# The beginning of a two-layer encoder: input pieces, weight halves and the order of the first copies

## The reference

```
def even_layer(x, norm_w, w_in, ...):
    h = rmsnorm(x, norm_w)
    proj = einsum('bsd,de->bse', h, w_in)          # 1024 x 9216
    qa, ka, va, ga, qh, ffw, fbw, ih, gh = split_cols(proj, EVEN_SIZES)
    oa = differential_attention(qa, ka, va, ..., cos, sin) * silu(ga)   # q, k rotated first
    ob = hgrn2_bidirectional(qh, ffw, fbw, ih, ...) * silu(gh)
    return einsum('bse,ed->bsd', concat([oa, ob]), w_out)
```

## Time and profile before

| | us |
|---|---|
| median of three runs | 1117.99 |
| the profiled execution, its own time | 1119.73 |
| its span, from the first instruction to the last | 1118.0 |
| PE busy | 1093.4 (98%) |
| DVE busy | 967.5 (87%) |
| ACT busy | 678.7 (61%) |

### The profile page before, as it was taken

One profiled execution on the slowest core, in us unless ns is written; L12 is line 12 of the kernel. 1 busy time (PEld: TensorE's weight loads), 2 busy tenths in 40 slices (PEclk: granted clock), 3 DMA queues, 4 the chain that ended last, 5 costly groups with the idle time before them and its releaser, 6 DMA issues. The chain is left out here.

```text
span 1118.0 us, 18504 instructions
## 1 busy us (share of the span) xinstructions
PE 1093.4 (98%) x5690; PEld 913.1 (82%) x5690; DVE 967.5 (87%) x1956; ACT 678.7 (61%) x1310; POOL 0.2 (0%) x4
## 2 busy tenths in 40 slices
PE   8999999999999999999999999999999999999996
PEld 7778878888888888888888867878888888888876
DVE  6879989889889889889889888888888888988886
ACT  6475665654654654654654765367677666677764
POOL 0000000000000000000000000000000000000000
PEclk9999999999999999999999999999999999999998
DMA  7614423324224224225125120563332324323111
GB/s 231 167 41 106 140 76 93 96 75 101 87 75 114 74 75 125 62 75 140 47 75 150 44 71 22 124 160 97 98 94 56 94 63 121 100 75 94 57 39 76
DMA packets 132634, 103.67 MB, mean 93 GB/s; under 512 B 5488, under 2 KB 118512, under 8 KB 132592
## 3 DMA queue, kind: packets, MB, share of 16 engines
q1 hardware_dynamic: 131760, 102.28, 33.4%
q10 hardware_dynamic: 832, 0.85, 0.2%
HBM read 77.95 MB, written 2.10 MB: 72 GB/s over the span
## 5 line engine op out<-in xcount | busy, mean ns | idle before, releaser
L75 PE MATMUL bank_proj<-hH,w_hi 128*128 128x512 f32 x856 | 341.4, 399 | 1.1 <-DVE w_lo L1323 1.1
L77 PE MATMUL bank_proj<-hH,w_lo 128*128 128x512 f32 x856 | 334.4, 391 | 0.0
L76 PE MATMUL bank_proj<-hL,w_hi 128*128 128x512 f32 x856 | 334.3, 391 | 0.0
L77 PEld LDWEIGHTS bank_proj<-hH,w_lo 128*128 128x128 f32 x856 | 160.8, 188 | 34.9
L75 PEld LDWEIGHTS bank_proj<-hH,w_hi 128*128 128x128 f32 x856 | 161.2, 188 | 32.2 <-DVE w_lo L1323 2.0
L76 PEld LDWEIGHTS bank_proj<-hL,w_hi 128*128 128x128 f32 x856 | 161.2, 188 | 29.8 <-issue 0.2
L2087 ACT ACTIVATE probs<-probs,small 128x256 f32<-128x256 f32 (+1 forms) x128 | 70.9, 556 | 55.2 <-DVE small L2355 54.8
L1323 DVE TENSOR_TENSOR w_lo<-w_raw,w_hi 128x1024 fp32r<-128x1024 f32 x73 | 88.3, 1218 | 0.9 <-ACT w_hi L789 0.9
L2094 ACT ACTIVATE probsT<-bank_odd_turn 128x256 fp32r<-128x256 f32 (+1 forms) x128 | 49.0, 434 | 64.4 <-PE bank_odd_turn L1810 63.7
L789 ACT ACTIVATE w_hi<-w_raw 128x1024 fp32r<-128x1024 f32 x73 | 76.9, 1053 | 0.2
L918 ACT ACTIVATE scaled<-decay 128x1024 f32<-128x1024 f32 x32 | 34.0, 1062 | 61.8 <-PE bank_score L611 59.7
(11 more groups left out here) (463 smaller groups left out, 2157.8 us busy)
## 6 DMA issues: line engine op xcount, KB each, us to landing
w_raw<-in_w_in_even SPq DMA_DIRECT2D x71, 512.0 KB, 4.7
w_raw<-in_w_in_odd SPq DMA_DIRECT2D x36, 512.0 KB, 4.9
qs<-parts SPq DMA_DIRECT2D x96, 128.0 KB, 2.4
ks<-parts SPq DMA_DIRECT2D x40, 256.0 KB, 4.5
o_raw<-in_w_out_even SPq DMA_DIRECT2D x15, 512.0 KB, 6.3
o_raw<-in_w_out_odd SPq DMA_DIRECT2D x14, 512.0 KB, 6.7
mixT<-in_x SPq DMA_DIRECT2D x4, 256.0 KB, 6.0
rope<-in_rope SPq DMA_DIRECT2D x2, 512.0 KB, 7.5
```

Of the source, the lines that this page charges most:

```text
L75: pe.matmul(out, hi, moving_hi, start=start, stop=False)
L76: pe.matmul(out, hi, moving_lo, start=False, stop=False)
L77: return pe.matmul(out, lo, moving_hi, start=False, stop=stop)
```

## The change

The change has five parts.

1. `x` comes in five pieces instead of four: of one, one, two, two and two tiles (`PIECES`). The first four pieces of rows 256 to 511 are issued by ACT, where before it issued the first two of four.
2. On SP's queue the third weight block (`load(0, 0)`) and the rotary tables are issued only after all of `x` has landed; the block now stands ahead of the tables.
3. The dummy matmuls are spread: seven ahead of tile 0, six ahead of tile 1, four ahead of tile 2, none ahead of tile 3. Tiles 4 to 7 are each turned behind one step of the first projection, where before tiles 4 and 5 stood together behind the first step.
4. The second weight block is split to high and low in two halves (`high_half`, `low_half`), and the first projection step of n = -1 waits for the first half alone. The second half of the first block moves behind tiles 2 and 3 on ACT and DVE.
5. `rotate(-1, 7)` takes `low(0, 1)` between its fourth and its fifth instruction; before, `low(0, 1)` stood behind it.

```diff
-WARM = 9
+WARM = (7, 6, 4, 0)
+PIECES = ((0, 1), (1, 2), (2, 4), (4, 6), (6, 8))
@@ sync
             load_half(0, half_landed)
             load_x(0, 1)
+            load_x(0, 2)
             load_half(4, w_in_sem[0])
-            for i in (2, 3):
-                for a in range(2):
-                    load_x(a, i)
+            load_x(0, 3)
+            load_x(0, 4)
+            load_x(1, 4)
             load(0, -1)
+            sp.wait_ge(x_landed[-1].sem, x_landed[-1].at(0, 2))
+            load(0, 0)
             sp.dma_start(rope[:], rope_d).then_inc(rope_landed.sem, DMA)
-            load(0, 0)
@@ tensor
-            for c in range(WARM):
-                pe.matmul(PB[1][:, 0:P], ones, ones, start=True, stop=True)
             for k in range(4):
+                for c in range(WARM[k]):
+                    pe.matmul(PB[1][:, 0:P], ones, ones, start=True, stop=True)
                 turn_x(k)
@@
-            proj(0, -2, 0, 1)
-            turn_x(4)
-            turn_x(5)
-            proj(0, -2, 1, 2)
-            turn_x(6)
-            proj(0, -2, 2, 3)
-            turn_x(7)
-            proj(0, -2, 3, 4)
+            for k in range(4):
+                proj(0, -2, k, k + 1)
+                turn_x(k + 4)
             proj(0, -2, 4)
-            proj(0, -1, 0, 5)
+            proj(0, -1, 0, 4)
+            proj(0, -1, 4, 5)
@@ scalar
-            for i in range(2):
+            for i in range(4):
...
             high_x(0)
             act.wait_ge(half_landed.sem, half_landed.at(0, 1))
-            act.activation(w_hi[0][:, 0:4], w_raw[0][:, 0:4], ACT.Copy).then_inc(half_high.sem, 1)
-            high_x(1)
+            high_half(0, 0, half_high)
+            for k in range(1, 4):
+                high_x(k)
             act.wait_ge(w_in_sem[0].sem, w_in_sem[0].at(0, 0))
-            act.activation(w_hi[0][:, 4:KT], w_raw[0][:, 4:KT], ACT.Copy).then_inc(w_high.sem, 1)
+            high_half(0, 4, w_high)
+            high_x(4)
             keep_first_x()
-            for k in range(2, KT):
+            for k in range(5, KT):
                 high_x(k)
-            high(0, -1)
+            act.wait_ge(w_in_sem[1].sem, w_in_sem[1].at(0, 0))
+            high_half(1, 0, half_high)
+            high_half(1, 4, w_high)
@@ vector, rotate
                 dve.tensor_tensor(turned[:, 0], turned[:, 0], turned[:, 1], ALU.add).then_inc(roped.sem, 1)
+                if between is not None:
+                    low(*between)
@@ vector
-            rotate(-1, 7)
-            low(0, 1)
+            rotate(-1, 7, between=(0, 1))
             rotate(-1, 8)
```

More of the change, by code:

```diff
@@ L230, in even_layer @@
         KEPT = (1, 2, 5, 3, 4)
-        x_landed = [sem(f"x_landed{i}", unit=DMA) for i in range(4)]
+        x_landed = [sem(f"x_landed{i}", unit=DMA) for i in range(len(PIECES))]
         eye_landed = sem("eye_landed", unit=DMA)
@@ L334, in load_x @@
             def load_x(a, i):
-                part = x[2 * a * P:2 * (a + 1) * P, 2 * i * P:2 * (i + 1) * P].rearrange("(t p) d -> p t d", p=P)
-                sp.dma_start(x_tiles[a][:, :, 2 * i * P:2 * (i + 1) * P], part).then_inc(x_landed[i].sem, DMA)
+                cols = slice(PIECES[i][0] * P, PIECES[i][1] * P)
+                part = x[2 * a * P:2 * (a + 1) * P, cols].rearrange("(t p) d -> p t d", p=P)
+                sp.dma_start(x_tiles[a][:, :, cols], part).then_inc(x_landed[i].sem, DMA)
             def load_half(first, count):
@@ L455, in turn_x @@
                     pe.wait_ge(eye_landed.sem, eye_landed.at(0, 1))
-                if k % 2 == 0:
-                    pe.wait_ge(x_landed[k // 2].sem, x_landed[k // 2].at(0, 2))
+                for i, (first, _) in enumerate(PIECES):
+                    if k == first:
+                        pe.wait_ge(x_landed[i].sem, x_landed[i].at(0, 2))
                 if k == 6:
@@ L476, in proj @@
                 bank, use = bank_of(n)
-                if n == -2 and first == 0:
-                    pe.wait_ge(half_low.sem, half_low.at(0, 1))
-                elif first == 0 or n == -2 and first <= 4 < end:
+                if n in (-2, -1) and first == 0:
+                    pe.wait_ge(half_low.sem, half_low.at(0, n + 3))
+                elif first == 0 or n in (-2, -1) and first <= 4 < end:
                     pe.wait_ge(w_low.sem, w_low.at(h, n))
@@ L762, in _ @@
         def _(act):
-            for i in range(2):
-                part = x[2 * P:4 * P, 2 * i * P:2 * (i + 1) * P].rearrange("(t p) d -> p t d", p=P)
-                act.dma_start(x_tiles[1][:, :, 2 * i * P:2 * (i + 1) * P], part).then_inc(x_landed[i].sem, DMA)
+            for i in range(4):
+                cols = slice(PIECES[i][0] * P, PIECES[i][1] * P)
+                part = x[2 * P:4 * P, cols].rearrange("(t p) d -> p t d", p=P)
+                act.dma_start(x_tiles[1][:, :, cols], part).then_inc(x_landed[i].sem, DMA)
                 if i == 0:
@@ L1349, in _, with low_half @@
             low_x = lambda k: raw.split_low(dve, k, XB[k][:])
+            def low_half(s, first, count):
+                part = slice(first, first + 4)
+                dve.tensor_tensor(w_lo[s][:, part], w_raw[s][:, part], w_hi[s][:, part].bitcast(F32),
+                                  ALU.subtract).then_inc(count.sem, 1)
             low_x(0)
             dve.wait_ge(half_high.sem, half_high.at(0, 1))
-            dve.tensor_tensor(w_lo[0][:, 0:4], w_raw[0][:, 0:4], w_hi[0][:, 0:4].bitcast(F32),
-                              ALU.subtract).then_inc(half_low.sem, 1)
-            low_x(1)
+            low_half(0, 0, half_low)
+            for k in range(1, 4):
+                low_x(k)
             dve.wait_ge(w_high.sem, w_high.at(0, -2))
-            dve.tensor_tensor(w_lo[0][:, 4:KT], w_raw[0][:, 4:KT], w_hi[0][:, 4:KT].bitcast(F32),
-                              ALU.subtract).then_inc(w_low.sem, 1)
+            low_half(0, 4, w_low)
             keep_x(KEPT[0])
-            for k in range(2, KT):
+            for k in range(4, KT):
                 low_x(k)
-            low(0, -1)
+            dve.wait_ge(half_high.sem, half_high.at(0, 2))
+            low_half(1, 0, half_low)
+            dve.wait_ge(w_high.sem, w_high.at(0, -1))
+            low_half(1, 4, w_low)
             for k in KEPT[1:]:
```

9 lines of the change are left out of this document (6 added, 3 removed).

## The result

The change makes the kernel slower by a little under 0.2%.

| | median | lowest to highest |
|---|---|---|
| before | 1116.86 us | 1116.0 to 1119.32 |
| after | 1119.36 us | 1117.94 to 1121.44 |

The account below looks back on a forecast made before the run. PE, busy 98% of the span, was taken to bound the kernel. Projection 2 starting 1.0 us later gave 1119.73 + 1.0 = 1120.7 us for the profiled execution and 1117.99 + 1.0 = 1119.0 for the median; range 1116.7 to 1120.7.

Parts of the forecast that it names:

- late `parts`: At the rotation, `parts` completes 1.13 us later, delaying the copies to L1246; projection 2 starts 1.0 us later.
- The landings of x: At the start, pieces land at 8.3 (tile 1), 9.9 (tiles 2 and 3) and 13.2 us (last).
- the gain at `scale_rope`: On DVE after the rotation's root, `scale_rope` starts at about 24.35 instead of 24.51, a gain of 0.15 us.
- the equal turns of the queues: Loads of x: engines alternate between queues packet by packet, so tile 1 lands at 8.2, tiles 2 and 3 at 9.7.
- the 0.2 that I added for shorter rows: Later landings of x: 0.2 us added for the shorter rows of the small pieces.
- Projection 1 started without a wait: On PE near 30.0 us, the earlier `low(0, 1)` removes the wait for `w_lo`, saving 0.64 us.
- The rival that feared a fall there: At the start, PE's clock falls to half from 9.9 us despite the dummies; 1120.1 us, chance 0.26.
- The pieces land early: Rival on x's loads: last piece lands by 11.6 us, projection 2 starts 0.5 to 0.7 earlier; 1117.4 us, chance 0.18.
- Nothing comes of it: Rival: an earlier rotation makes up for the late `parts`, or PE's later stalls swallow it; 1118.0 us, chance 0.14.
- The clock falls at 9.4: Rival on PE's clock at the start: half clock for tiles 2 and 3, 2.1 us later; 1120.1 us, chance 0.26.

Follow-up runs that it names:

- e1_no_between: The changed kernel with `low(0, 1)` behind `rotate(-1, 7)` again, as before the change; 1117.59 us, ratio 1.0000 to before.
- e2_only_between: The kernel before with only the move of `low(0, 1)` into `rotate(-1, 7)`; 1119.02 us, ratio 1.0014 to before.
- e4_dummies_first: e1_no_between with nine dummy matmuls all ahead of tile 0 and none later; 1119.61 us, ratio 1.0026 to before.
- e5_dummies_in_wait: The changed kernel with five dummy matmuls on PE ahead of the transposes of `vt`; 1118.61 us, ratio 1.0009 to before.
- e8_old_tile_order: e1_no_between with tiles 4 to 7 turned in the old order; 1117.53 us, ratio 1.0005 to before.
- e12_no_hold: e8_old_tile_order with rotary tables and third weight block loaded in the old order, without waiting for x; 1117.35 us, ratio 1.0002 to before.
- e11_new_pieces_only: The kernel before with only the five new pieces of x on their new queues and the spread dummies; 1116.38 us, ratio 0.9992 to before.

## Why the prediction was right, and where it was not

**The step that decided, late `parts`: right.** Forecast: L1246 waits 1.7 us for the copies, `vt` and `low(0, 2)` come 1.0 later, PE waits from 35.6 to 37.0 and again to 38.1. Measured: 1.52 us, and waits of 1.21 + 0.41 us. `parts` complete to L1246 is 4.4 us as before. With equal beginnings (second profiles) the move costs 1.04 us up to projection 2 and 0.99 up to the scores; e1_no_between and e2_only_between show it by itself. The loss is still there at the later mark: the first stall after projection 2 starts at 65.68 in after's second profile, at 64.89 in before's.

**The landings of x and the gain at `scale_rope`, mis-sized.** I put tile 1 at 8.3, tiles 2 and 3 at 9.9, and tile 7 on ACT at 15.7 to 15.9. In the profile they are at 7.54, 9.04 and 14.92 (in others up to 9.69 and 15.67). I had added up bytes ahead on both queues and taken the upper end for tiles 2 and 3. By the equal turns of the queues that the Trainium skill ("DMA: Bandwidth & Descriptors", section on queues, rings and completion order) describes I had reckoned 8.2 and 9.7; tiles 2 and 3 landed up to 0.9 before that too, and no run here tells the two reckonings apart. Nor does one show the 0.2 that I added for shorter rows. Before itself had them at 8.84 in its second profile and 9.17 in the first. The gain at `scale_rope` I put at 0.15 us. In the first profiles it is 1.04, of which most is the half clock in before's; between the second profiles it is 0.09, and after's second was an early execution (1117.76, against the 1118.63 of its undisturbed runs). By the times of e1_no_between the undisturbed beginning costs 1.0 us, where the sum had a gain. Projection 1 started without a wait, as forecast, and that win was lost again at projection 2.

**The clock: half right.** The forecast had it stay full at the start, and it did. The rival that feared a fall there did not come about, and e4_dummies_first shows that the dummies prevent it; the window from 9.43 is at 1.00. The Trainium skill ("TensorE: Matmul & The Clock Gate", part 4) says that transposes do not count as work for the clock the way matmuls do; e4_dummies_first fell with the same transposes that e1_no_between kept its clock with, which agrees as far as the dummies decide. My reading that this rule would bring the fall here, with 1.6 us of dummies to count, was wrong. What I did not see is that the wait I had worked out at `vt` and `w_lo` could let the clock fall too, although rows 8 showed a fall behind a stretch with PE idle for 1.5 of 3.41 us, and my own sum had PE wait for most of 35.6 to 38.1. I priced the wait at its length alone. Its second price, 1.6 us in the executions in which the clock falls there, is missing from the sum.

**The comparison's base.** I moved the profiled 1119.73 by the sum and subtracted the same 1.74 to come to the median. But the first profile of before holds two falls (at 9.20 and at 654.33) while 68 of 100 runs keep a mean clock of 0.997 or more: its span is 2.8 us above that of the second profile, 1.1 of it up to the scores and 1.7 behind them. So what the beginning repairs was hardly in before's median. The three runs were high as well: their median is 1117.99, that of all eighteen 1116.86. That 1119.0 came so near the measured 1119.36 is therefore in part luck: the base was 1.1 too high and the step from it 0.8 to 1.5 too small.

**The sum over runs.** Between undisturbed runs: 1.0 for the move of `low(0, 1)` (e5_dummies_in_wait 1118.61 less e1_no_between 1117.59) and 1.1 for the beginning (1117.59 less 1116.53), together the 2.1 that is measured, as they must be, since after's undisturbed runs have the median of e5_dummies_in_wait; the second is 1.0 against the runs on e1_no_between's own chip. Half of after's runs are below 0.997 and 1.4 us longer (+0.7), a third of before's are and 2.0 us longer (-0.6). That gives 2.2, between the 1.8 of the ratio and the 2.5 of the two medians. The forecast had the first term right; the second it had as a gain of 0.15 at `scale_rope`, and the third not at all.

**The rivals.** "The pieces land early" gave 1117.4. In after's first profile the last piece landed at 12.3, just above the 12.0 that would have decided for it, and ACT took tile 7 at 14.92, below the 15 that I had named as a mark against the forecast; yet the time went up, since the copies of `parts` and the clock took more than the early tile gave. "Nothing comes of it" (1118.0) is excluded: the interval begins at +1.1 us. "The clock falls at 9.4" was wrong in its place, and its price for one fall was 1.1 us, as much as before's first profile, with the fall at 9.20, trails its second at the scores; 1.6 was paid at 38.24.

**What stays open.** How the 1.0 us between the undisturbed beginnings divides between the halves on ACT, the tile order and the landings of x: the traces show 0.4 and 0.3 to 0.5 for the first two. The times of e8_old_tile_order show nothing for the order; those of e12_no_hold beside e11_new_pieces_only point to the halves. The kernel that would decide, after with neither the halves nor the move, and after's order and held loads kept, was not run. It is also open which executions of a kernel lose the clock behind the same wait.

## What to carry to other kernels

Before an instruction is put between two that complete a buffer, ask which transfer hangs on the second and whether its consumer already waits: here 1.13 us put there came out again as 1.0 us, while the wait that it removed was 0.63 by the distance of starts, and was not on the path. A wait of PE has two prices, its length and the clock that may fall behind it, and a few dummy matmuls remove the second where they fill time in which PE waits anyway. Look at the mean clock of every run before you argue from one profile, and take a second one: a part that repairs what at most one execution in three suffers is worth at most a third of what the profile says.

## What the runs showed of the hardware

The clock fell to half behind waits of PE much shorter than the stretch it then lasted (3.41 us each time): after 1.21 + 0.41 us at 38.24, and after 2.14 us at 43.78. The same waits did not bring a fall in after's second profile (1.23 + 0.41) nor in that of e2_only_between (1.21 + 0.41), nor 1.69 us in before's second. Five dummy matmuls in the wait, 1.28 us on PE, kept it in 12 of 12 runs. Five profiles with the same beginning had tiles 2 and 3 turned at 8.76 to 9.69 us, so a landing at the start of a kernel is known no better than half a us either way.
